# A 512-token encoder trunk in split fp32: mean and root of one norm by pairs of token tiles

## What is computed

```
mix = jnp.concatenate([a, r], axis=-1) @ w_o[i]
x = x + rmsnorm(mix, norm_mix_post[i])
h = rmsnorm(x, norm_mlp_pre[i])
m = jnp.square(jax.nn.relu(h @ w_up[i])) @ w_down[i]
x = x + rmsnorm(m, norm_mlp_post[i])
```

## Time and profile before

| | before |
|---|---|
| median of 3 runs | 1527.02 us (1525.15 to 1527.42) |
| profiled execution | 1527.86 us |
| its span, first to last instruction | 1525.9 us |
| TensorE matmuls busy | 1483.3 us, 97% |
| weight loads | 1212.9 us, 79% |
| VectorE | 654.7 us, 43% |
| ScalarE | 545.3 us, 36% |
| GpSimd | 662.7 us, 43% |
| mean granted TensorE clock | 0.992 |

### The profile page before, as it was taken

One profiled execution on the slowest core, in us unless ns is written; L12 is line 12 of the kernel. 1 busy time (PEld: TensorE's weight loads), 2 busy tenths in 40 slices (PEclk: granted clock), 3 DMA queues, 4 the chain that ended last, 5 costly groups with the idle time before them and its releaser, 6 DMA issues.

```text
span 1525.9 us, 18912 instructions
## 1 busy us (share of the span) xinstructions
PE 1483.3 (97%) x7192; PEld 1212.9 (79%) x7192; DVE 654.7 (43%) x908; ACT 545.3 (36%) x1020; POOL 662.7 (43%) x539
## 2 busy tenths in 40 slices
PE   6999998999999999999999999999999999999998
PEld 5878888778747778877888888888888888888876
DVE  6134555546476675255513223230412233361465
ACT  5223233123245555344423233332323333343452
POOL 3373636345200002445445455454545555554481
PEclk9999999899999999999999999999999999999999
DMA  5221110012240002522333333333233333332252
GB/s 193 63 63 42 27 37 21 11 35 56 63 97 1 1 1 97 173 83 76 118 97 97 98 97 97 97 99 95 96 99 99 97 95 101 91 123 92 82 164 85
DMA packets 82954, 124.31 MB, mean 81 GB/s; under 512 B 14641, under 2 KB 31025, under 8 KB 82865
## 3 DMA queue, kind: packets, MB, share of 16 engines
q1 hardware_dynamic: 82864, 123.11, 26.4%
HBM read 116.79 MB, written 4.19 MB: 79 GB/s over the span
## 4 chain that ended last, share of the span: by engine, by line
PE 92%; DVE 3%; POOL 2%; issue 1%; ACT 1%; DMA 0%; SPq 0%; DVEq 0%; POOLq 0%; ACTq 0%
PE ps L50 25%; PE ps L52 24%; PE ps L51 24%; PE ps L909 3%; PE ps L1430 3%; PE ps L1448 3%; PE ps L1438 2%; PE ps L1290 2%; PE ps L1000 1%; PE ps L939 1%; PE ps L954 1%; POOL wx_low L365 1%; PE ps L885 0%; PE ps L965 0%; PE ps L995 0%
## 5 line engine op out<-in xcount | busy, mean ns | idle before, releaser
L1225 POOL TENSOR_TENSOR wy_low<-w_raw,wy_high 128x512 fp32r<-128x512 f32 x320 | 442.8, 1385 | 436.6 <-ACT wy_high L1205 436.6
L1205 ACT ACTIVATE wy_high<-w_raw 128x512 fp32r<-128x512 f32 x320 | 202.1, 632 | 559.9 <-PE ps L52 556.2
L50 PE MATMUL ps<-a_high,wy_high 128*128 128x512 f32 x512 | 200.2, 391 | 0.0
L52 PE MATMUL ps<-a_high,wy_low 128*128 128x512 f32 x512 | 199.5, 390 | 0.0
L51 PE MATMUL ps<-a_low,wy_high 128*128 128x512 f32 x512 | 199.4, 390 | 0.0
L50 PE MATMUL ps<-wy_high,hid_high 128*128 128x512 f32 x512 | 199.4, 389 | 0.0
L52 PE MATMUL ps<-wy_high,hid_low 128*128 128x512 f32 x512 | 199.2, 389 | 0.0
L51 PE MATMUL ps<-wy_low,hid_high 128*128 128x512 f32 x512 | 199.2, 389 | 0.0
L365 POOL TENSOR_TENSOR wx_low<-w_raw,wx_high 128x512 fp32r<-128x512 f32 (+1 forms) x64 | 82.3, 1290 | 142.3 <-ACT wx_high L466 142.3
L52 PEld LDWEIGHTS ps<-a_high,wy_low 128*128 128x128 f32 x512 | 96.2, 188 | 20.1
L51 PEld LDWEIGHTS ps<-a_low,wy_high 128*128 128x128 f32 x512 | 96.4, 188 | 19.9
(11 more groups left out here) (196 smaller groups left out, 2500.4 us busy)
## 6 DMA issues: line engine op xcount, KB each, us to landing
w_raw<-in_w_up SPq DMA_DIRECT2D x128, 256.0 KB, 2.7
w_raw<-in_w_down SPq DMA_DIRECT2D x128, 256.0 KB, 2.6
w_raw<-in_w_in SPq DMA_DIRECT2D x62, 256.0 KB, 2.8
w_raw<-in_w_o SPq DMA_DIRECT2D x32, 256.0 KB, 2.7
w_raw<-in_w_ple_gate SPq DMA_DIRECT2D x32, 256.0 KB, 2.6
x_tile<-in_x SPq DMA_DIRECT2D x8, 512.0 KB, 8.2
x_res<-in_x SPq DMA_DIRECT2D x8, 512.0 KB, 6.2
y<-x_res SPq DMA_DIRECT2D x16, 256.0 KB, 2.1
```

The costliest lines, as they stand in the source:

```text
L50: pe.matmul(out, stat_high, mov_high, start=start, stop=False)
L52: return pe.matmul(out, stat_low, mov_high, start=False, stop=stop)
L1205: act.activation(out, w_raw[:, q % RING, :], ACT.Copy).then_inc(high_made, 1)
L1225: pool.tensor_tensor(low_tile, w_raw[:, q % RING, :], high_tile.bitcast(F32), ALU.subtract).then_inc(low_made, 1)
```

## The change

Mean and root of this norm are made for two token tiles at a time. VectorE makes the first mean of a half behind the third addition, then does the fourth addition and goes straight to the first normed tile; the second mean stands behind the second normed tile. GpSimd's roots for the pairs stand behind the low parts made at chunks 3 and 5, where one root for four stood at chunk 4. The normed tile waits for the root of its own pair.

```diff
@@ pool_tail
-                        if (s, k) == ((2, U00)[h], 4):
-                            roots_of(mean7x_made, h + 1, mean7x, rstd7x, rstd7x_made, four)
+                        if s == (2, U00)[h] and k in (3, 5):
+                            two = slice(4 * h + k - 3, 4 * h + k - 1)
+                            roots_of(mean7x_made, two.start // 2 + 1, mean7x, rstd7x, rstd7x_made, two)
@@ dve_tail
-                def means7x(h):
-                    four = slice(4 * h, 4 * h + 4)
-                    dve.wait_ge(squared7x, 4 * h + 4)
-                    dve.tensor_scalar(mean7x[:, four], ssq7x[:, four], 1.0 / D, EPS, ALU.mult,
+                def means7x(t):
+                    two = slice(t, t + 2)
+                    dve.wait_ge(squared7x, t + 2)
+                    dve.tensor_scalar(mean7x[:, two], ssq7x[:, two], 1.0 / D, EPS, ALU.mult,
                                       ALU.add).then_inc(mean7x_made, 1)
 
                 def tile7(t):
-                    dve.wait_ge(rstd7x_made, t // 4 + 1)
+                    dve.wait_ge(rstd7x_made, t // 2 + 1)
@@
                     sums7(h)
-                    for t in range(4):
+                    for t in range(3):
                         add7(o + t)
-                    means7x(h)
+                    means7x(o)
+                    add7(o + 3)
                     if h == 0:
                         dve.wait_ge(pre_in, 16)
                     tile7(o)
                     tile7(o + 1)
+                    means7x(o + 2)
                     low_of(dve, 1, o)
```

## The result

| | before | changed |
|---|---|---|
| median | 1527.02 us (5 runs) | 1518.32 us (1517.14 to 1519.47, 5 runs) |
| ratio to before | | 0.9946, 95% interval 0.9932 to 0.9961 |
| profiled execution, span | 1527.86, 1525.9 us | 1519.47, 1517.5 us |

The change saves 8.7 us by the medians; 8.4 had been forecast. In two later groups of runs the changed kernel gave 0.9946 (0.9934 to 0.9959) and 0.9949 (0.9937 to 0.9962).

The account below looks back on a forecast made before the run. TensorE, 92% of the chain that ended last, was taken as the bound, so only its waits and lower clock could be won: 9.02 us less 0.64 left, net 8.4, from 1527.02 to 1518.6 us; range 1516.8 to 1521.4.

Parts of the forecast that it names:

- Which time was to be won: TensorE's waits at both half boundaries before the transposes, with the slower clock behind them: 4.52 and 4.50, together 9.02 us.
- The mean's place: VectorE, first half: the first mean, issued at 654.48 inside a low part on GpSimd, ends about 655.27 us.
- Root and addition collide: GpSimd's first root is held by VectorE's fourth addition and ends 0.57 us behind it, at 657.03; chance 0.50.
- The estimate for two columns: GpSimd's root of two columns takes 0.70 us, on the line between one (0.55) and four (1.01).
- The rival without a collision: GpSimd's root runs unhindered beside the fourth addition, both waits before the transposes vanish: 1518.0 us; chance 0.27.
- First normed tile: VectorE, first half: it ends at 659.34 instead of 661.88 us, leaving TensorE 0.32 us of wait before the transposes.
- The mis-sized term: Loss left at the two boundaries, TensorE's wait before the transposes alone: 2 x 0.32 = 0.64 us.
- Clock: TensorE at both boundaries: a wait of 0.3 us brings no clock fall, so 1.66 and 1.63 us are won whole.
- The rival "within 0.2%": VectorE loses its turn to a second low part, 2 x 1.58 us of wait plus clock falls: 1524.5 us; chance 0.04.
- both clock terms: Time lost to TensorE's lower clock behind the wait at each boundary: 1.66 and 1.63 us, 3.3 in this rival's sum.
- Second mean and root: Added on VectorE and GpSimd in each half, cost nothing: next segment's first low part done at 663.8, wanted at 665.6.
- Total: Whole kernel: 9.02 us won less 0.64 left gives net 8.4 us, a median of 1518.6 us.

Follow-up runs that it names:

- one-boundary kernel: Changed kernel with pairs in the first half only, the second half as before: ratio 0.9969 to the kernel before, median 1522.10 us.

## Why the prediction held

- **Which time was to be won.** Right: 4.52 and 4.50 us a boundary, wait and clock together, and nothing else. The one-boundary kernel gives it one by one, and behind 745 us each matmul of the changed kernel starts 8.30 to 8.35 us ahead of the same one before, both counted from the last matmul ahead of the first transposes.
- **The mean's place.** Right: issued at 654.41 into a low part, ended 0.03 us behind it at 655.20 (655.27 forecast, and all of this execution is 0.07 earlier).
- **Root and addition collide.** Right, and it was the one step of this walk that no row had shown: 1.67 us in the addition's presence, 0.70 without, and its end 0.57 us behind the addition, as forecast. The estimate for two columns, 0.70 between the 0.55 of one and the 1.01 of four, was met. The rule cited from the Trainium skill, "SBUF — State Buffer", section "Who interferes with whom", agrees with this: two-input VectorE work and a GpSimd instruction that reads SBUF took turns, root included. The mean, which has one input only, was held as well (0.79 against 0.16 us); that sentence does not speak of it, the forecast took it from a row. The rival without a collision falls.
- **First normed tile.** Right: its end was forecast at 659.34 and measured at 659.29; wait 0.32 forecast, 0.35 and 0.36 measured.
- **The mis-sized term.** The loss that stays at a boundary was put at the wait alone, 2 x 0.32 = 0.64. The matmuls behind a wait start a little later too (0.85 us from transposes to matmul where the undisturbed ones have 0.80), and it is 0.39 + 0.40 = 0.79.
- **Clock.** Right in its result: 1.00 over both boundaries. The reason given was thinner than it looked. It rested on one idle time of 2.56 us with no fall. That one holds in every profile taken (2.55 or 2.56 before the same matmul, no fall), but at the boundaries an idle time of 2.41 and 2.40 us brought the fall, and one of 1.88 once of two. So the length of a wait alone does not decide; what else does stays open. What the runs bear out is that waits of 0.35 to 1.48 us at the boundaries brought no fall in any profile; 0.35 lies well inside.
- **The rival "within 0.2%".** It added a second low part to the wait, and both clock terms with it. The run with the root at chunk 4 had such a wait (1.48 and 1.46 us) and no fall: it lost 2.2 us, not 5.9.
- **Second mean and root.** Right to call them free: the low part was done at 663.62 (forecast 663.8), wanted at 665.76 (25th matmul behind the transposes), 2.1 us of cover.
- **Total.** 8.4 us forecast; 8.23 at the boundaries, 8.30 to the last matmul, 8.7 by the medians. That the medians come within 0.3 of the forecast says little, since the interval of the ratio spans 0.0029, or 4.4 us. The boundaries are the firmer check.

## What to carry to other kernels

Where the bottleneck engine waits at the end of a serial chain of reduce, root and scale, cut the reduction to what the first consumer needs, and walk the chain engine by engine together with the background work that holds up the same engines: here that walk gave the finish of the first tile to 0.05 us. Count the clock with the wait: at the boundaries here, six of seven waits of 2.0 to 2.9 us cost 1.6 us beyond themselves, and those of 1.5 us or less at most 0.05. A small instruction that waits in an in-order queue is free only while what stands behind it has cover; beyond the cover each microsecond is paid in full.

## What the runs showed of the hardware that was not expected

- The same wait gave two outcomes for the clock in one execution: 2.04 us with a fall, 2.03 without (both 1.88 idle). And 2.56 us of idle time in an earlier stage brought no fall where 2.40 brought one here. Behind the wait of 2.04 us the fall showed only after TensorE had started again: transposes at 658.58, the wider spacing of the matmuls from 660.06.
- Part of the spread from execution to execution is made long before the changed place. Granted clock in the stretch from 262 to 278 us, first the profile of the changed kernel, then that with the fourth addition ahead of the mean, the same code up to there:

```profile
262.00:278.00 16.00, 13.76 (x51) 12.32 (x52) 1.22 (x3) 3.10 (x6) 0.00 (x0) 0.57 0.00 1
```

```profile
262.00:278.00 16.00, 14.96 (x66) 13.34 (x66) 0.02 (x1) 1.94 (x3) 0.00 (x0) 0.68 0.00 1
```

  At the first boundary they stand at 658.77 and 656.51 us. So spans of two profiles cannot be subtracted to find an effect of one microsecond; distances within a trace, from a matmul before the change to one behind it, can.
- Of a VectorE and a GpSimd instruction that start 0.02 us apart (653.35 and 653.37), the later one by the record went first. The start of a record can lie up to 0.08 us before the end of the one ahead of it on the same engine, so it does not tell whose turn it is.
